# Two weight tiles per row behind each norm, last squares summed in PSUM, and a down projection that waits row by row: a four-layer transformer kernel on Trainium2

## What is computed

```python
# first block, 2 layers (context is updated in layer 0 alone)
h = rms_norm(x, norm_g) * (1 + scale) + shift          # scale, shift, gate = silu(c) @ w_mod + b_mod
p = h @ w_in                                           # 3072 columns: fourier, pool, q, k, v, gate
x = x + gate * (concat(fourier, pool, differential_attention) * silu(g)) @ w_out
# second block, 2 layers; sh, sc, g = silu(c) @ ada_w + ada_b
h = rms_norm_2(x, norm1_w) * (1 + sc1) + sh1
x = x + g1 * (concat(retention, hgrn2) of (h @ w_in)) @ w_out
h = rms_norm_2(x, norm2_w) * (1 + sc2) + sh2
a = h @ w_gate                                         # 1024 -> 2816, causal convolution of width 3 on a
x = x + g2 * (silu(conv(a)) * (h @ w_val)) @ w_down
return rms_norm_2(x, final_norm_w)
```

## Time and profile before

| | |
|---|---|
| median of 3 runs | 2362.05 us (2358.32 to 2367.21) |
| profiled execution, its own time | 2361.11 us |
| its span, first to last instruction | 2359.8 us |
| mean granted TensorE clock | 0.959 |
| PE / PE weight load busy | 92% / 74% |
| DVE / ACT / POOL busy | 56% / 34% / 36% |
| DMA | mean 102 GB/s |

### The profile page before, as it was taken

The page is one execution under the profiler, slowest core; times in us unless marked ns, Lnnn a source line. Parts: engine busy times, 40 slices in busy tenths (PEclk is TensorE's granted clock), DMA queues, the critical chain, the costliest instruction groups (busy, mean ns, idle before and its releaser), DMA issues.

```text
span 2359.8 us, 25946 instructions
## 1 busy us (share of the span) xinstructions
PE 2168.6 (92%) x10488; PEld 1750.0 (74%) x10488; DVE 1332.7 (56%) x1580; ACT 801.0 (34%) x1124; POOL 849.9 (36%) x458
## 2 busy tenths in 40 slices
PE   6999989988999986999998999998899998999998
PEld 2678877775777764788876878876788886878876
DVE  4476667564556744584366732866475375741545
ACT  2345555313555523323323312322323323322321
POOL 0331123323322443433234444543432244444442
PEclk9999999988999997999999999999999998999999
DMA  7321211223222233533233433531532232442332
GB/s 264 116 81 54 72 54 59 59 70 126 89 72 72 80 107 115 175 108 107 63 90 98 152 95 103 169 114 55 178 118 97 81 90 80 138 122 79 98 104 75
DMA packets 313446, 240.88 MB, mean 102 GB/s; under 512 B 6768, under 2 KB 289520, under 8 KB 312688
## 3 DMA queue, kind: packets, MB, share of 16 engines
q1 hardware_dynamic: 294176, 169.48, 24.4%
q0 software_dynamic: 18432, 67.12, 8.3%
q10 hardware_dynamic: 720, 2.62, 0.3%
HBM read 237.10 MB, written 2.10 MB: 101 GB/s over the span
## 4 chain that ended last, share of the span: by engine, by line
PE 79%; DVE 7%; issue 5%; ACT 4%; POOL 2%; DMA 2%; SPq 0%; DVEq 0%; ACTq 0%; POOLq 0%
PE ps L515 61%; PE ps L1881 2%; PE ps L977 1%; PE ps L1009 1%; PE ps L863 1%; PE ps L1615 1%; PE ps L982 1%; ACT a_p L1236 1%; POOL w_lo_second L498 1%; PE ps L1020 1%; DMA first_mod<-in_w_mod_first 1%; POOL w_lo_first L498 1%; PE ps L1862 1%; DVE attention_stats L1412 1%; DVE norm_second_tmp L680 1%
## 5 line engine op out<-in xcount | busy, mean ns | idle before, releaser
L498 POOL TENSOR_TENSOR w_lo_second<-w_raw_second,w_hi_second 128x1024 fp32r<-128x1024 f32 (+1 forms) x200 | 514.9, 2575 | 768.8 <-ACT w_hi_second L492 768.8
L515 PE MATMUL ps<-h_second_hi,w_hi_second 128*128 128x512 f32 x1216 | 495.3, 407 | 38.6 <-POOL w_lo_second L498 15.8
L515 PE MATMUL ps<-h_second_lo,w_hi_second 128*128 128x512 f32 x1216 | 480.1, 395 | 0.0
L515 PE MATMUL ps<-h_second_hi,w_lo_second 128*128 128x512 f32 x1216 | 480.1, 395 | 0.0
L492 ACT ACTIVATE w_hi_second<-w_raw_second 128x1024 fp32r<-128x1024 f32 (+1 forms) x200 | 221.3, 1107 | 389.9 <-PE ps L515 381.4
L515 PEld LDWEIGHTS ps<-h_second_hi,w_hi_second 128*128 128x128 f32 x1216 | 232.1, 191 | 104.0 <-POOL h_second_lo L738 20.5
L498 POOL TENSOR_TENSOR w_lo_first<-w_raw_first,w_hi_first 128x1024 fp32r<-128x1024 f32 x64 | 161.3, 2521 | 305.8 <-ACT w_hi_first L492 304.8
L515 PEld LDWEIGHTS ps<-h_second_hi,w_lo_second 128*128 128x128 f32 x1216 | 232.2, 191 | 49.9
L515 PEld LDWEIGHTS ps<-h_second_lo,w_hi_second 128*128 128x128 f32 x1216 | 232.7, 191 | 47.3 <-issue 1.9
L515 PE MATMUL ps<-h_hi,w_hi_first 128*128 128x512 f32 (+1 forms) x640 | 250.9, 392 | 16.6 <-POOL h_lo L738 7.4
L515 PE MATMUL ps<-h_hi,w_lo_first 128*128 128x512 f32 (+1 forms) x640 | 230.6, 360 | 0.0
(11 more groups left out here) (271 smaller groups left out, 3466.9 us busy)
## 6 DMA issues: line engine op xcount, KB each, us to landing
w_raw_second<-in_w_in SPq DMA_DIRECT2D x64, 512.0 KB, 5.5
w_raw_first<-in_w_in SPq DMA_DIRECT2D x48, 512.0 KB, 3.8
mod_w_mixer<-in_ada_w_turned POOLq DMA_DIRECT2D x48, 512.0 KB, 5.0
w_raw_second<-in_w_gate SPq DMA_DIRECT2D x44, 512.0 KB, 5.3
w_raw_second<-in_w_val SPq DMA_DIRECT2D x44, 512.0 KB, 3.9
w_raw_second<-in_w_down SPq DMA_DIRECT2D x32, 704.0 KB, 4.8
mod_w_ffn<-in_ada_w_turned POOLq DMA_DIRECT2D x29, 512.0 KB, 4.9
mod_w_in<-in_w_mod_turned POOLq DMA_DIRECT2D x28, 512.0 KB, 3.9
```

The lines of the kernel that those rows point to most:

```text
L498: k.nc.gpsimd.tensor_tensor(lo, raw, hi.bitcast(F32), ALU.subtract).then_inc(k.sem.weight_split, 1)
L515: last = tensor.matmul(k.ps[:, bank, 0:count], w[:, cut], x[q][:, first:first + count], start=(q == 0 and n == 0), stop=(q == t.k - 1 and ...
```

## The change

- **Pairs.** Behind each norm but the last the first two tiles of the stage are multiplied together, row by row (`multiply_pair`). Both are rounded and split ahead of the norm; the loops start rounding and splitting with the third. In the first block the side work of steps 0 to 5 comes after the pair, that of 6, 7 and 8 in the third tile. The second tile of layer 0 has banks 7 and 2.
- **Squares.** In norms over 512 tokens (calls 2 to 6) the last row's square is no longer added by DVE; PE sums the seven added rows, then adds the last square in the same PSUM places, in banks 2 to 5; the roots are spread in bank 6.
- **Root table.** A root of one column stands ahead of the wait for the sums, so the table is loaded there.
- **Down.** PE waits for each row of the activations apart (`ffn_ready`).
- **Moved.** The layer vectors are made ahead of the last residual; the lower bounds in the first layer; modulation sums: six instead of seven beside the out stage of layer 1, one instead of four at tile 3 of in2, two at tile 13 (layer 0) or 9, 13 and 17 (layer 1), twelve instead of nine in layer 0's first ffn stage.

The core of the diff:

```diff
-        for i in range(1, 8):
+        for i in range(1, 7):
             second(("out", 1), i)
         for l in (0, 1):
-            for i in range(24):
-                second(("in2", l), max(i, 3))
+            for i in sorted([*range(3, 24), *((13,) if l == 0 else (9, 13, 17))]):
+                second(("in2", l), i)
             for half in (0, 1):
-                for i in sorted([*range(4, 22, 2), *((5, 9, 13) if l == 0 and half else ())]):
-                    if n < (96 if l else 64):
+                for i in sorted([*range(4, 22, 2), *(() if l else (5, 9, 13))]):
+                    if n < 96:
                         second(("ffn", l, half), i)
...
+def multiply_pair(k, u, ready):
+
+    for q in range(k.tiles[u].k):
+        for v in (u, u + 1):
+            for p in range(len(k.tiles[v].parts)):
+                multiply_rows(k, v, p, (q,), ready)
...
-def linear_gpsimd(k, stage, then):
+def linear_gpsimd(k, stage, then, first=0):
...
-        if u != own[-1] or then:
+        if i >= first and (u != own[-1] or then):
             split_tile(k, u + 1)
...
+def linear_tensor(k, stage, ready=None, pair=False):
+    own = k.stage_tiles[stage]
+    if pair:
+        multiply_pair(k, own[0], ready)
+    for i, u in enumerate(own):
+        if i >= (2 if pair else 0):
+            multiply_tile(k, u, ready if i == 0 else None)
...
-        if u != own[-1] or then:
+        if i >= first and (u != own[-1] or then):
             round_tile(k, u + 1)
...
+        if last and u == own[-1]:
+            last()
...
+    squared = vector.tensor_tensor(square, x, x, ALU.mult)
+    if n == KT - 1 and cut == X_:
+        squared.then_inc(k.sem.last_squared, 1)
+        return
+    settle_vector(k, squared)
     added = vector.tensor_tensor(k.ssq[:, cut], k.ssq[:, cut], square, ALU.add)
-    if last:
+    if n == (KT - 2 if cut == X_ else KT - 1):
         added.then_inc(k.sem.squares_summed, 1)
...
+    return k.ps[:, 6, 0:t // P] if t > TX else k.ps[:, 2:6, 0]
...
+    return k.banks(4, t) if t > TX else k.banks(6, t)
...
     for q in range(t // P):
-        last = tensor.matmul(k.ps[:, 6, q:q + 1], k.ssq[:, q * P:(q + 1) * P], k.ones[:, 0:1], start=True, stop=True)
+        last = tensor.matmul(sums[:, q:q + 1], k.ssq[:, q * P:(q + 1) * P], k.ones[:, 0:1], start=True, stop=not apart)
+    if apart:
+        tensor.wait_ge(s.last_squared, call - 1)
+        for q in range(t // P):
+            last = tensor.matmul(sums[:, q:q + 1], k.square2[:, q * P:(q + 1) * P], k.ones[:, 0:1], start=False, stop=True)
...
+    scalar.activation(k.small[:, 60:61], k.eps[:, 0:1], ACT.Sqrt)
     scalar.wait_ge(k.sem.norm_summed, call + 1)
-    scalar.activation(k.roots[:, 0:t // P], k.ps[:, 6, 0:t // P], ACT.Sqrt, bias=k.eps[:, 0:1],
+    scalar.activation(k.roots[:, 0:t // P], norm_sums(k, t), ACT.Sqrt, bias=k.eps[:, 0:1],
...
+    multiply_pair(k, k.stage_tiles["in", l][0], ready)
+    for s in range(6):
+        first_products(k, l, s)
     for i, u in enumerate(k.stage_tiles["in", l]):
+        if i < 2:
+            continue
         both = len(k.tiles[u].parts) == 2
         for p in range(len(k.tiles[u].parts)):
             def side(q):
                 point = POINTS[0 if both else 1].get((p, q))
                 if point is not None:
-                    first_products(k, l, 4 * i + point)
-            multiply_rows(k, u, p, range(KT), ready if i == p == 0 else None, side)
+                    for s in (6, 7, 8) if i == 2 and point == 0 else (4 * i + point,):
+                        first_products(k, l, s)
+            multiply_rows(k, u, p, range(KT), None, side)
...
-            round_tile(k, own[i] + 1)
+            if i:
+                round_tile(k, own[i] + 1)
...
+    multiply_pair(k, own[0], ready)
     for i, u in enumerate(own):
-        multiply_tile(k, u, ready if i == 0 else None, lambda q: q == 3 and mixer_tensor_middle(k, l, i))
-        mixer_tensor_end(k, l, i)
+        if i >= 2:
+            multiply_tile(k, u, None, lambda q: q == 3 and mixer_tensor_middle(k, l, i))
+            mixer_tensor_end(k, l, i)
...
-        round_tile(k, u + 1)
+        if i:
+            round_tile(k, u + 1)
...
+    def ready(q):
+        k.nc.tensor.wait_ge(k.sem.ffn_low, (2 * l + half) * FFH + q + 1)
+    return ready
...
-            linear_tensor(k, ("ffn", l, half), norm_ready(k, 3 + 2 * l) if half == 0 else None)
-            k.nc.tensor.wait_ge(k.sem.ffn_low, (2 * l + half + 1) * FFH)
-            linear_tensor(k, ("down", l, half))
+            linear_tensor(k, ("ffn", l, half), norm_ready(k, 3 + 2 * l) if half == 0 else None, half == 0)
+            linear_tensor(k, ("down", l, half), ffn_ready(k, l, half))
...
     for l in range(2):
-        layer_vectors(k, l, 0)
...
-        linear_vector(k, ("out2", l), second_residual(k, l, G1, True))
-        layer_vectors(k, l, 1)
+        linear_vector(k, ("out2", l), second_residual(k, l, G1, True), lambda: layer_vectors(k, l, 1))
...
-            linear_vector(k, ("down", l, half), second_residual(k, l, G2, half == 1))
+            linear_vector(k, ("down", l, half), second_residual(k, l, G2, half == 1),
+                          (lambda: layer_vectors(k, 1, 0)) if l == 0 and half else None)
...
         if l:
+            round_tile(k, first_tile(k, ("in", 1)) + 1)
...
         round_tile(k, first_tile(k, ("in2", l)))
+        round_tile(k, first_tile(k, ("in2", l)) + 1)
...
+        round_tile(k, first_tile(k, ("ffn", l, 0)) + 1)
...
-            linear_scalar(k, ("ffn", l, half), True, ffn_scalar(k, l, half), None if half else (3, 4 + 2 * l))
+            linear_scalar(k, ("ffn", l, half), True, ffn_scalar(k, l, half), None if half else (3, 4 + 2 * l), 1 - half)
```

71 lines of the change are left out of this document (41 added, 30 removed).

## The result

The changed kernel takes **2299.67 us** (median of 4 runs, 2297.40 to 2301.53) against 2364.63 us before in the same comparison (2358.32 to 2369.84): a ratio of **0.9729**, 95% interval 0.9710 to 0.9748. The profiled execution took 2297.4 us with a span of 2296.1, so 63.7 us less than the profiled one before, at a mean granted clock of 0.970 instead of 0.959.

What follows compares the result with a forecast made beforehand. TensorE was taken as the bound, with time to win only where it idles: 22 + 0.7 + 9 + 13 - 0.8 + 0.5 - 1 = 43.4 us off the profiled 2361.1, forecast 2318 us, range 2306 to 2331.

Steps and rivals of the forecast that it cites:

- Down by row: Four down projection starts: waiting per row removes the gaps and the half clock behind them, 22 us.
- The waits of the pair: Second-block norms: third tile waits 3.8 us (ffn) or 4.0 (input projection); the fifth input tile waits 1.7.
- Costed at nothing: … lower bounds: Layer vectors and lower bounds: small DVE work, now under other waits, so 0 us.
- I take half clock behind it: Behind the third tile's wait at second-block norms: 1.8 us of half clock, leaving 4.5 net per ffn norm.
- the new gaps leave the clock alone: Rival, chance 0.15: six half-clock stretches fall away, four of 1.8 us and two of 1.7, giving 2307 us.
- A gap of 1.7 with half clock as before: Fifth tile of the second block's input projection: the wait shrinks from 5.24 to 1.7 us, half clock stays behind it.
- doubled loads in layer 1: Layer 1 input projection, tiles 9, 13 and 17: at 9 the second load waits for a late sum, 0.8 us lost.
- The norm chain: Three 512-token norms: last add and root table load leave the chain, 0.7 + 1.3 = 2.0 us each.
- The square and its port: Rival, chance 0.06: POOL's split blocks DVE's last square, 2.4 us at three norms, 2325; forecast had the square start first.
- First block: Norms of 768 tokens: 0.5 us gained in layer 1, 1 lost in layer 0.

Runs made afterwards that it cites:

- a_all64: The changed kernel with every buffer of the second block, weights and activations alike, 32 bytes higher: 2301.33 us, ratio 0.9743 to before.
- a_chunks: The changed kernel with the modulation sums of layer 1's input projection back where they were before the change: 2307.47 us, ratio 0.9768 to before.
- a_pad: The changed kernel with 32 bytes left free in front of mixed, act_hi and act_lo, so they stand where they stood before: 2314.68 us, ratio 0.9797 to before.

## Why the prediction was right and wrong

- **Down by row: right**, term and mechanism: 22.0 against 22, and 22.2 when done alone.
- **The waits of the pair: right to 0.3 us** (3.56, 3.93 and 1.65 against 3.8, 4.0 and 1.7). That the third tile waits because it needs what the first tile holds is shown by a_third, which gives it buffers and a bank of its own; which of them counts most was not tried.
- **"Costed at nothing: … lower bounds": this step failed**, and is the largest miss, 9.3 of 20.4 us. The edit was read as an instruction that moves; it also moves three buffers. The evidence was in the trace of before: the prediction noted 5.5 us for a tile of 24 and 7.6 for one of 33, but took both for the same 0.23 us. 33 products of 0.2267 are 7.5 us, those of 0.2333 are 7.7.
- **"I take half clock behind it": missed in the profiled execution, right in most others.** At the ffn stages 7.7 were gained against 5.0, since no half clock stood behind 3.56 us. With the same order a_all64 and a_chunks had it, and their stages give 4.9 us each. So the pair was sized right and the 2.7 us are the luck of the clock. The rival "the new gaps leave the clock alone" (0.15, 2307) came true in the ffn stages alone; that with the place of the buffers on top it gives 2298, near the 2299.67, is chance: behind the third tile's wait in the input projections half clock stands in every run of this order.
- **"A gap of 1.7 with half clock as before": this step failed.** The input projections gained 14.5 against 10.2. Up to the fifth tile's start the stages gained 4.2 and 4.1 us, as forecast (4.2 each). Behind its 1.65 us no half clock stands, in the changed kernel or in any kernel made from it, where it stood behind the old wait: from there to their ends the stages gained another 1.7 and 1.3 us. The 0.8 us taken off for the doubled loads in layer 1 do not show (both stages are 264.5 us long), and the second block starts 0.4 sooner than forecast.
- **The norm chain: mechanism right, size off**: 8.9 against 6.0. The missing part is the spreading passes at full clock, 0.9 of 2.1 us at a norm. (One of the three chains was half clocked again in a_all64, and 1.5 us longer.) The prediction counted the waits in the chain and took the passes as fixed.
- **The square and its port: right** where forecast. At the three norms with a table load the square starts 0.31 to 0.34 us ahead of POOL and is through in 0.69. The rival came true at the one norm of the first block where nobody looked: 2.0 us at the add.
- **First block: inside its noise.** The 0.8 us won there mean nothing beside 4 us between equal runs.
- The range failed because every unknown was taken as a delay that stays or goes. None of the cases let the steady pace of the products change, so the lower end stood at 2306. Of the 20.4 us missed, 9.3 are the pace and some 8.5 the clock: 2.8 in the spreading passes, 3.0 behind the fifth tile, 2.7 behind the third tile in the ffn stages.

## What to carry to other kernels

Where a kernel is bound by one engine, read its steady pace stage by stage before its idle times: two paces under the same instructions and the same granted clock are a finding, and an edit that allocates or frees a few bytes ahead of matmul operands is an edit of that pace. A pause costs more than its length, and less predictably: passes and products behind it may run at half clock, so shortening a chain also speeds up what stands in it. And when a tile is prepared earlier, ask which buffer the tile after next now waits for; here a third buffer gave another 14 us.

## What the runs showed of the hardware

- The pace of a matmul of 128 by 512 (float32 bits, rounded operands) depends on how its moving and stationary operands lie to each other in SBUF. Alike modulo 256: 0.2267 us (0.2278 in the first block's out stage). 64 bytes off: 0.2286. 32 or 128 bytes off: 0.2333. Moving both by 32 bytes changes nothing. Other offsets weren't tried.
- The same wait is followed by half clock in one place or run and not in another: behind 3.56 us the granted clock was 1.00 in the changed kernel and 0.50 in a_pad, whose order of work is the same:

```profile
1250.00:1256.40 6.40, 5.44 (x13) 4.28 (x14) 3.90 (x3) 1.37 (x2) 3.28 (x2) 0.50 0.75 221
```

- ACT's table load takes 1.28 us, and the root behind it starts 0.01 to 0.02 us later.
- A split of 2.5 us on POOL that starts 0.3 to 0.4 us before an add on DVE makes the add of 0.69 or 0.96 us take 2.7 to 3.0.
